# A gated delta-rule recurrence in 128-token block-diagonal tiles, rebuilt on 64x64 tiles per chunk and head

## The reference, cut to what matters

```python
def step(state, inp):                       # state: 64x64 for each of 8 heads
    r_t, w_t, k_t, v_t, kk_t, a_t = inp
    sa = einsum('bhvk,bhk->bhv', state, -kk_t)
    state = state * w_t + sa * (kk_t * a_t) + v_t * k_t
    return state, einsum('bhvk,bhk->bhv', state, r_t)
_, y = lax.scan(step, state0, ...)          # 512 tokens
mean = jnp.mean(y, axis=-1, keepdims=True)
var = jnp.mean(jnp.square(y - mean), axis=-1, keepdims=True)
y = ((y - mean) * lax.rsqrt(var + GN_EPS)).reshape(B, S, RWKV_WIDTH) * ln_w + ln_b
y = (y + bonus) * g
```

## Time and profile before

| | |
|---|---|
| median of 3 runs | 1519.2 us (1518.49 to 1520.52) |
| span of the profiled execution | 1517.9 us |
| its own time, outside the profiler's view | not recorded; the median lies 1.3 us above the span |
| TensorE busy | 1472.5 us, 97% |
| VectorE, ScalarE, GpSimd busy | 562.3, 501.6, 781.5 us |
| HBM read | 154.1 MB, 103 GB/s over the span |

### The profile page before, as it was taken

How to read it: one execution, slowest core, us unless ns; L and a number is a source line. 1 busy time by engine, 2 the same in 40 slices (tenths; PEclk the granted TensorE clock), 3 DMA queues, 4 the chain that set the end, 5 groups by cost and what they waited for, 6 DMA issues and landing times.

```text
span 1517.9 us, 20105 instructions
## 1 busy us (share of the span) xinstructions
PE 1472.5 (97%) x7240; PEld 1222.1 (81%) x7240; DVE 562.3 (37%) x794; ACT 501.6 (33%) x687; POOL 781.5 (51%) x1028
## 2 busy tenths in 40 slices
PE   7999999999999999999999999889899999999997
PEld 6877888888888788888888788778777888888887
DVE  6976422221005722222000779835535222221003
ACT  6334333333114432323212673222334232322112
POOL 1662755555556654555555756441355454555553
PEclk9898999999999999999999999989999999999999
DMA  9872433232221333232322222000122323232221
GB/s 367 313 299 84 138 111 109 84 107 91 99 94 67 102 107 109 84 110 83 111 97 97 74 70 78 21 1 1 40 87 84 110 84 109 83 111 97 97 69 56
DMA packets 45557, 156.93 MB, mean 103 GB/s; under 512 B 5057, under 2 KB 8513, under 8 KB 45377
## 3 DMA queue, kind: packets, MB, share of 16 engines
q1 hardware_dynamic: 45504, 156.22, 30.1%
HBM read 154.10 MB, written 2.10 MB: 103 GB/s over the span
## 4 chain that ended last, share of the span: by engine, by line
PE 83%; DVE 9%; issue 3%; ACT 3%; POOL 1%; DMA 0%; DVEq 0%; SPq 0%; POOLq 0%; ACTq 0%
PE ps L1739 25%; PE ps L1740 25%; PE ps L1741 25%; DVE tri_p L1148 1%; DVE tri_x L1148 1%; POOL w_lo L515 1%; PE ps L2165 1%; DVE mid_sq L1151 1%; PE ps L2221 1%; PE ps L2172 1%; PE ps L2178 0%; ACT w_hi L706 0%; DVE pads L1148 0%; PE ps L2225 0%; PE ps L2119 0%
## 5 line engine op out<-in xcount | busy, mean ns | idle before, releaser
L515 POOL TENSOR_TENSOR w_lo<-raw,w_hi 128x256 fp32r<-128x256 f32 x932 | 695.4, 779 | 589.8 <-ACT w_hi L706 588.6
L1739 PE MATMUL ps<-act_hi,w_hi 128*128 128x512 f32 x1328 | 524.8, 395 | 4.1 <-DVE act_lo L1151 2.6
L1740 PE MATMUL ps<-act_lo,w_hi 128*128 128x512 f32 x1328 | 518.3, 390 | 0.0
L1741 PE MATMUL ps<-act_hi,w_lo 128*128 128x512 f32 x1328 | 518.2, 390 | 0.0
L706 ACT ACTIVATE w_hi<-raw 128x1024 fp32r<-128x1024 f32 x233 | 245.0, 1055 | 433.7 <-PE ps L1741 411.5
L1739 PEld LDWEIGHTS ps<-act_hi,w_hi 128*128 128x128 f32 x1328 | 250.3, 188 | 60.9 <-issue 4.9
L1740 PEld LDWEIGHTS ps<-act_lo,w_hi 128*128 128x128 f32 x1328 | 250.4, 189 | 53.0 <-issue 2.2
L1741 PEld LDWEIGHTS ps<-act_hi,w_lo 128*128 128x128 f32 x1328 | 250.1, 188 | 52.5
L1739 PE MATMUL ps<-hid_hi,w_hi 128*128 (+2 forms) x588 | 220.3, 375 | 2.6 <-DVE hid_lo L1148 1.7
L1740 PE MATMUL ps<-hid_lo,w_hi 128*128 (+2 forms) x588 | 220.1, 374 | 0.0
L1741 PE MATMUL ps<-hid_hi,w_lo 128*128 (+2 forms) x588 | 220.1, 374 | 0.0
(11 more groups left out here) (284 smaller groups left out, 1114.7 us busy)
## 6 DMA issues: line engine op xcount, KB each, us to landing
raw<-weight_units SPq DMA_DIRECT2D x233, 512.0 KB, 3.3
wm_mid<-mod_units SPq DMA_DIRECT2D x18, 512.0 KB, 9.0
wm_ring<-mod_units SPq DMA_DIRECT2D x14, 512.0 KB, 8.5
wm_early<-mod_units SPq DMA_DIRECT2D x8, 512.0 KB, 7.7
wm_late<-mod_units SPq DMA_DIRECT2D x8, 512.0 KB, 8.6
x_tok<-tokens SPq DMA_DIRECT2D x4, 512.0 KB, 6.1
xT<-tokens_by_channel SPq DMA_DIRECT2D x1, 2048.0 KB, 8.3
result<-act_out SPq DMA_DIRECT2D x16, 128.0 KB, 1.8
```

The source lines that it names most:

```text
L515: ins = nc.gpsimd.tensor_tensor(w_lo[:, slot, c], raw[:, slot, c], w_hi[:, slot, c].bitcast(f32), SUB)
L1739: nc.tensor.matmul(o, wh, xh, start=start, stop=False, **check)
L1740: nc.tensor.matmul(o, wh, xl, start=False, stop=False, **check)
L1741: return nc.tensor.matmul(o, wl, xh, start=False, stop=stop, **check)
```

## The change

All per-token products of the recurrence are made of 64x64 tiles, one for each chunk and head: the half of the array's rows by which a chunk (or head) is stored, by the half of its output partitions. No cross-chunk block is computed, and the masks, TT, X, S and K's results shrink to half.

- V is multiplied by a centring matrix (identity minus 1/64 within a head) while it is transposed, by matmuls in place of transposes. The mean product and its subtraction are gone.
- K is made before LR, in one step; G1, W, GH, MT, N are one step each; tB and tK are transposed after G1, and VectorE copies K's transpose.
- N stays in PSUM: the state products accumulate onto it, and VectorE only scales the sum by the decay. State 0 is scaled by ScalarE. RP and OV are one step, RO, after state 1. OV stays in PSUM, and Y accumulates onto it.
- bc is a transpose. The mask comes in two DMAs. The S tiles are not cleared, the four TT and X tiles are half as large and cleared in one place.
- `LAG` is 7 instead of 10, `AHEAD_OF_SOLVE` 3 instead of 4; the pair's program has 17 turns instead of 20. GpSimd's and ScalarE's waits in the closing part are on RO and Y instead of Nb, OV and S6.

The core of the diff:

```diff
-LAG = 10
+LAG = 7
-AHEAD_OF_SOLVE = 4
+AHEAD_OF_SOLVE = 3
...
+PE_STEPS = (["tV", "tA", "K", "LR", "AV", "G1", "tB", "tK", "W", "GH", "MT", "N", "S1", "RO"]
+            + [f"S{c}" for c in range(2, NCH - 1)] + ["Y", "var", "bc"])
+VE_STEPS = (["KA", "KR", "LR", "AVb", "G1b", "tK", "Wb", "GHb", "MT", "S1", "S2", "RP"]
+            + [f"S{c}" for c in range(3, NCH - 1)] + ["y", "inv", "yn"])
+AC_STEPS = ["tV", "tA", "AVa", "G1a", "tB", "Wa", "GHa", "S0", "bias", "sq", "sd", "wide"]
...
-            sp.dma_start(sumsq[:, 0:NMASK], a_mask[:, P:P + NMASK]).then_inc(sem("loaded_masks"), 16)
+            for o in range(2):
+                q = slice(o * CH, (o + 1) * CH)
+                sp.dma_start(masks[q], a_mask[q, P:P + NMASK].rearrange("p (k t) -> p k t", t=P)[:, :, q]).then_inc(sem("loaded_masks"), 16)
...
+                stt(cent, bones, -1.0 / HS, ident, MUL, ADD, "centre")
...
+                for name, g in (("KA", 0), ("KR", 1)):
+                    pe_did("K")
+                    did(name, nc.vector.tensor_tensor(
+                        b.MK[:, g, :, :, :], ps[:, b.bank + 2:b.bank + 4, :].rearrange("q h (c g t) -> q h c g t", c=NCP, g=2)[:, :, :, g, :],
+                        over_chunks(masks[:, g, :], NCP), MUL))
...
+                    did(f"S{c}", nc.vector.tensor_scalar(b.S[:, c, :], bank(2 + c % 2)[:, o:o + HS], pchunk[:, p, c:c + 1], None, MUL, ALU.bypass))
...
+                did("y", nc.vector.tensor_copy(y.rearrange("q (c o t) -> q o c t", o=2, t=CH), by_half(0, HALF)))
...
+                for c in range(NCP):
+                    cols = slice(c * P, (c + 1) * P)
+                    last = nc.tensor.matmul(bank(0)[:, cols], rV[:, p, cols], cent, start=True, stop=True)
+                did("tV", last)
...
+                for c, o, cols in CHUNKS:
+                    for h, r in enumerate(heads):
+                        last = nc.tensor.matmul(bank(2 + h)[halves[o], c * P:(c + 1) * P], rK[r, p, cols], rAR[r, :, p, cols], start=True, stop=True)
+                did("K", last)
...
+                def chunk_products(k, width, lhs, rhs, start):
+
+                    for swap in range(2):
+                        for n, (c, h) in enumerate(SYSTEMS):
+                            for half in range(2):
+                                q, c_ = halves[half ^ swap], c + 2 * half
+                                last = nc.tensor.matmul(bank(k + half)[q, n * width:(n + 1) * width], lhs(q, c_, h), rhs(q, c_, h), start=start and n == 0, stop=True, skip_group_check=n > 0 or not start)
+                    return last
...
+                did("G1", chunk_products(0, P, lambda q, c, h: b.TT[q, h * NCP + c, :], lambda q, c, h: b.AA[q, c, h, :], True))
+                token_major("tB", rB, 2)
+                token_major("tK", rK, 3)
...
+                for c in range(NCP):
+                    for o, q in enumerate(halves):
+                        for h, r in enumerate(heads):
+                            last = nc.tensor.matmul(ps[r, b.bank + o, c * CH:(c + 1) * CH], b.GH[q, 0, 2 * c + h, :], tok(b.BT, c, q, h), start=True, stop=True)
+                did("MT", last)
...
+                def state(c):
+                    o = c // 2 * HS
+                    did(f"S{c}", nc.tensor.matmul(bank(2 + c % 2)[:, o:o + HS], b.MT[:, c, :], b.S[:, c - 1, :], start=False, stop=True, skip_group_check=True))
...
+                for n in range(2 * (NCH - 1)):
+                    h, c = Y_ORDER[n]
+                    r = heads[h]
+                    o = HALF + c // 2 * CH
+                    last = nc.tensor.matmul(ps[r, b.bank + c % 2, o:o + CH], b.S[r, c - 1, :], b.RP[r, c * CH:(c + 1) * CH], start=False, stop=True, skip_group_check=True)
+                did("Y", last)
```

More of the change, by code:

```diff
@@ L663, in pair @@
                         pooling(g, WINDOWS[g])
-                for _ in range(16):
+                for _ in range(13):
                     yield
@@ L2149, in pair @@
[L2149 to L2166 removed]
+                halves = [slice(o * CH, (o + 1) * CH) for o in range(2)]
@@ new lines, in pair @@
+                did("K", last)
+                yield
+                ac_did("tV")
+                ac_did("tA")
+                for c, o, cols in CHUNKS:
+                    for h, r in enumerate(heads):
+                        last = nc.tensor.matmul(bank(h)[halves[o], c * CH:(c + 1) * CH], rB[r, p, cols], rR[r, p, cols], start=True, stop=True)
+                did("LR", last)
+                yield
+                SYSTEMS = [(c, h) for c in range(2) for h in range(2)]
+                def chunk_products(k, width, lhs, rhs, start):
[5 more added lines that the diff above has]
+                    return last
@@ L2215, in pair @@
-                yield
-                ve_did("Nb")
-                after(sem("cleared"), cleared_through(f"S{p % 2}"))
-                for c in range(1, NCH - 1):
-                    if c > 1:
-                        ve_did(f"S{c - 1}")
-                    did(f"S{c}", nc.tensor.matmul(bank((c + 1) % 2)[:, 0:P], b.MT[:, c, :], b.S[:, c - 1, :], start=True, stop=True))
+                    for lhs, rhs, first in ((lambda q, h: tok(b.BT, c, q, h), lambda q, h: b.GH[q, 1, 2 * c + h, :], True), (lambda q, h: tok(b.KT, c, q, h), lambda q, h: tok(b.VT, c, q, h), False)):
+                        for o, q in enumerate(halves):
+                            for h, r in enumerate(heads):
+                                last = nc.tensor.matmul(ps[r, b.bank + 2 + o, c * HS:(c + 1) * HS], lhs(q, h), rhs(q, h), start=first and c == 0, stop=not first, skip_group_check=c > 0)
@@ new lines, in pair, with state @@
+                did("N", last)
+                yield
+                def state(c):
+                    o = c // 2 * HS
+                    did(f"S{c}", nc.tensor.matmul(bank(2 + c % 2)[:, o:o + HS], b.MT[:, c, :], b.S[:, c - 1, :], start=False, stop=True, skip_group_check=True))
+                ac_did("S0")
+                ve_did("MT")
+                state(1)
+                for c in range(NCP):
+                    for o, q in enumerate(halves):
+                        for h, r in enumerate(heads):
+                            last = nc.tensor.matmul(ps[r, b.bank + o, c * CH:(c + 1) * CH], b.GH[q, 0, 2 * c + h, :], b.MBR[q, h, c, :], start=True, stop=True)
@@ new lines, in pair @@
+                for c in range(NCP):
+                    for lhs, rhs, first in ((lambda q, h: b.GH[q, 1, 2 * c + h, :], lambda q, h: b.MBR[q, h, c, :], True), (lambda q, h: tok(b.VT, c, q, h), lambda q, h: b.MK[q, 1, h, c, :], False)):
+                        for o, q in enumerate(halves):
+                            for h, r in enumerate(heads):
+                                last = nc.tensor.matmul(ps[r, b.bank + o, HALF + c * CH:HALF + (c + 1) * CH], lhs(q, h), rhs(q, h), start=first and c == 0, stop=not first, skip_group_check=c > 0)
@@ L2226, in pair @@
                 did("Y", last)
-                yield
-                ve_did("Y")
-                did("mean", nc.tensor.matmul(bank(0), bones, rB[:, p, :], start=True, stop=True))
                 yield
@@ L2237, in pair @@
                 for t in range(TT_):
-                    last = nc.tensor.matmul(bank(2)[:, t * P:(t + 1) * P], rK[:, p, t * P:(t + 1) * P], ident, start=True, stop=True)
+                    last = nc.tensor.transpose(bank(3)[:, t * P:(t + 1) * P], rK[:, p, t * P:(t + 1) * P], ident)
                 did("bc", last)
```

324 lines of the change are left out of this document (126 added, 198 removed).

## The result

The changed kernel takes 1492.4 us (median, 1491.6 to 1493.2) against 1518.9 for the kernel before on the same chip (four executions of each; the three shown above had a median of 1519.2): a ratio of 0.982 [0.981, 0.983]. Forecast were 1487 us and 32 us gained; 26.5 were gained. The profiled execution's span fell from 1517.9 to 1491.1 us.

What follows compares the result with a forecast made beforehand. TensorE bounds the kernel, busy 97% of the span. In the stage (pair 0's first transpose to the end of 21 output-projection blocks), 32.3 products - 3.2 shape changes + 3 waits = 32 us; 1519.2 - 32 = 1487, range 1475 to 1505.

Steps and rivals of the forecast that it cites:

- the case that was called likeliest: The forecast's own case: a time of 1480 to 1497 us, chance 0.58.
- The products: TensorE's products in the stage: 22.7 us a pair before, 14.6 after; 32.3 us saved for four pairs.
- The term of the waits: TensorE's waits in the stage, from start to start: 20.5 us against about 23, so 3 us less.
- the clock: Low clock in the stage: about 6 us lost before, and the same 6 us taken for after.
- the state products: State products on TensorE stay as they are: a narrower moving operand does not shorten the step set by the weight load.
- changes of shape: Changes between tile shapes on TensorE: five more a pair, 0.8 us a pair, 3.2 us in all, between 0 and 9.
- The opening: From 968 us to pair 0's G1: G1 starts at about 981.9 instead of 985.4, with 6.3 us of waits.
- the woven part: Where pairs are interleaved on TensorE: twelve waits of 0.4 to 1.0 us, some 8 us.
- Pair 0 alone: Waits before pair 0's W, GH, MT and states 1, 3 and 4: sum 4.9 us.
- Outside the stage: Everything before 968 us and after the 21 output blocks was to stay as it was.
- The rival of a longer low clock: Clock at 0.50 for 20 to 50 us more, costing half of itself: 1497 to 1512 us; chance 0.21.
- the turn of the sign: The change turns slower where low clock covers over 76 us of the stage's roughly 115.

Runs made afterwards that it cites:

- e4: Changed kernel with all 64x64 tiles of a quadrant following one another instead of quadrants taking turns; 1547 to 1597 us, median 1570.
- e1: Changed kernel with one more wait: GpSimd's pooling starts when the inverse of the triangles is done; 1490.6 us.
- e6: Changed kernel with GpSimd's pooling waiting for the inverse and ScalarE copying pair 0's blocks before pair 1's AV; 1486.6 us.
- e5: Changed kernel with 4 matmuls of 512 columns, result overwritten, put before pair 1's AV to fill TensorE's wait; 1488.9 us.
- e8: Changed kernel with the centring undone: V transposed as it is, mean product and subtraction after Y; 1501.4 us.
- e10: e6 with LAG 4 instead of 7, and GpSimd waiting for its own X in every pair; 1502.8 us.

## Why the prediction was right, and which steps of it were off

The time fell into the range and into the case that was called likeliest. The products, the carrier of the forecast, came out as said. The term of the waits did not: 3 us less were said and 6 more came, 9 us apart, and the total stayed as near as it did partly by luck. The stage gained 28.5 us. Of that 29.6 are products (22.7 to 15.3 us a pair), -6 the waits, some 2 the clock, in which the forecast saw no gain, and some 1.4 the state products, said to stay as they were (two instructions, 0.49 us in the earlier trace rows, take 0.43 now). The last two and the remaining 1.5, which no row places, the sum did not have. Point by point:

- **Products: right.** 14.6 us a pair and 0.8 for changes of shape were said, 15.3 measured; 15 and 30 ns from start to start came out as 16 (RO: 1.56 us for 96) and 32 (K: 1.03 for 32), scaled from a gram of 64 columns. The quadrants have to take turns for that, which e4 tests.
- **The opening: a wait that the forecast had too short.** The stage gained 147.8 - 119.3 = 28.5 us, 3.5 short of the forecast, and 2.4 of these are the opening: G1 was to start 13.9 us behind the stage's start and came at 16.3. "GpSimd clears four half-size tiles and none of S, so its pooling can start earlier, which nothing waited for" was the false sentence. Nothing waits for it, but it runs beside VectorE's last steps of the inverse and holds them; in the kernel before it began at 983.6 us, behind the clearing of S and so behind the inverse. Of the "2 us less ahead of the inverse" on VectorE only 1.0 was left: it was done 10.7 us behind the stage's start, 11.7 before, and 9.3 in e1. And with pair 1's AV late, the queue order on ScalarE, known and named, kept its price. With both repaired (e6) G1 comes at 12.4 and the way is 6.5 us shorter.
- **Waits: said to fall by 3 us, and rose.** TensorE's idle time went from 15.3 us in 23 pieces (the prediction took some 30, which made its 23 us from start to start 2 too many) to 21.4, also in 23: 6 us more. From start to start that is some 27 where 20.5 were said. Beside the opening it is the woven part: 8.6 us in 13 pieces, some 12 from start to start with 0.25 of modelled tail each, where 8 were said. Pair 0 alone has 4.1 in 6 pieces, 5.6 so counted, for 4.9 said.
- **The clock: nearly as said**, 13.6 us low against 17.1, but elsewhere: the woven part ran at 1.00 throughout, and the loss hung on the opening. By half of TensorE's busy time in the low stretches, an estimate, the loss is 5.3 us where it was 7.5, so the clock gave back some 2 of the 6 us of longer waits. There a stall was priced by its length alone; e5 shows that its company, the low clock on G1, cost as much.
- **Outside the stage** 402 us follow in both kernels, as said. Its start came 1.96 us later, 0.3 of it by a longer wait just ahead (1.20 us for 0.89). The rest arose in the first 200 us, in unchanged code, and is left unexplained; the starts of the other programs spread by more. With the 3.5 us it makes the 5.5 by which the gain fell short.
- **The rival of a longer low clock was the one to fear.** e4, e8 and e10, each a small edit, had 174, 31 and 34 us at the low clock. The prediction put the turn of the sign at 76 us; e4, beyond it, is slower than the kernel before, though part of that is its slower products, so it does not test that turn by itself.

## What to carry to other kernels

Small products pay when neighbours in the queue lie in different quadrants of the array: write the loops so that quadrants take turns, and read the start-to-start distance in the trace. When an engine is freed early, ask which engine it will now run beside, not only who waits for it. Close a wait of TensorE in thin work before anything else, since the clock may fall with it, and what follows then takes nearly twice as long (G1: 1.96 and 3.68 us); but once only a few us of low clock are left, filling one place moved them to another and won nothing.

## What the runs showed of the hardware

- **A VectorE step with two SBUF inputs waits for GpSimd's to end.** The step on 60 columns (976.34, 0.79 us) ended at 977.13, GpSimd's (975.76, 1.29) at 977.05; the one on 31 columns (977.42, 1.06) at 978.48, GpSimd's (977.39, 1.04) at 978.43. In e1, with GpSimd silent, they took 0.21 and 0.19 us. The Trainium skill, SBUF — State Buffer, section "SBUF: two separate sides", says that a VectorE operation with two SBUF inputs and a GpSimd operation that reads SBUF exclude each other for a whole instruction; the trace agrees, to 0.08 us.
- **64x64 tiles over four quadrants start every 15 to 16 ns** (64 columns) and 30 ns (128 columns); with all of a quadrant in a row K took 74 ns, and starts of different quadrants overtake the order of the queue (e4).
- **The clock is a matter of what TensorE did before**: it fell to 0.50 behind a wait of 3.7 us after thin products, stayed at 1.00 when that wait was filled, and with a few instructions more (e8) or another order (e4) stood at 0.50 for 31 and 174 us. The same G1 took 1.90 to 1.96 us at the one level and up to 3.7 at the other. What part of such a longer low time comes from the waits and what from the thinner work, no run separates.
